# Triangular inverse of a gated DeltaNet block: one shared weight matrix per tile for two heads, transposes for the third product

## What is computed

```python
m = jnp.where(strict_lower, jnp.einsum("bhncd,bhnsd->bhncs", k_beta, k) * decay, 0.0)
t_inv = lax.linalg.triangular_solve(eye + m, jnp.broadcast_to(eye, m.shape),
                                    left_side=True, lower=True, unit_diagonal=True)
u = jnp.einsum("bhncs,bhnsd->bhncd", t_inv, v_beta)
w = jnp.einsum("bhncs,bhnsd->bhncd", t_inv, k_beta * jnp.exp(g)[..., None])
```

## Time and profile before

| | us |
|---|---|
| median of three runs | 2079.56 |
| lowest, highest | 2065.73, 2081.7 |
| span of the profiled execution | 2082.3 |
| TensorE busy | 1965.2 (94%) |
| VectorE busy | 1376.5 (66%) |
| ScalarE busy | 815.7 (39%) |
| GpSimd busy | 655.2 (31%) |
| first and last matmul of the inverse | 128.3, 659.7 |

### The profile page before, as it was taken

How to read it: one execution, slowest core, us unless ns; L and a number is a source line. 1 busy time by engine, 2 the same in 40 slices (tenths; PEclk the granted TensorE clock), 3 DMA queues, 4 the chain that set the end, 5 groups by cost and what they waited for, 6 DMA issues and landing times. The chain is left out here.

```text
span 2082.3 us, 30616 instructions
## 1 busy us (share of the span) xinstructions
PE 1965.2 (94%) x11569; PEld 1751.7 (84%) x11569; DVE 1376.5 (66%) x2764; ACT 815.7 (39%) x1260; POOL 655.2 (31%) x682
## 2 busy tenths in 40 slices
PE   8999999999998799998998989999989999999999
PEld 7776677677666588898998979999989999999999
DVE  5542542532531564299899998888667787778777
ACT  4333433433432443242433336656533333333332
POOL 4133033032031100058987841322212222222221
PEclk9999999999998899999999999999999999999999
DMA  3210210210200642259997968888779999999997
GB/s 115 79 49 21 71 37 11 71 36 21 82 16 6 230 152 89 83 150 311 309 341 263 311 197 304 311 313 307 257 253 319 319 318 322 319 319 319 320 319 239
DMA packets 147986, 411.79 MB, mean 198 GB/s; under 512 B 15616, under 2 KB 63872, under 8 KB 147328
## 3 DMA queue, kind: packets, MB, share of 16 engines
q1 hardware_dynamic: 109056, 269.31, 37.4%
q0 software_dynamic: 38784, 140.53, 20.5%
HBM read 360.23 MB, written 49.55 MB: 197 GB/s over the span
## 5 line engine op out<-in xcount | busy, mean ns | idle before, releaser
L1417 ACT ACTIVATE expert_hi<-raw 128x1024 fp32r<-128x1024 f32 x288 | 305.4, 1061 | 423.9 <-PE psE L86 392.5
L84 PE MATMUL psE<-x2h,expert_hi 128*128 128x384 f32 x1024 | 349.5, 341 | 15.3 <-POOL expert_lo L1536 14.0
L84 PE MATMUL psE<-w_hi,expert_hi 128*128 128x384 f32 x1024 | 351.2, 343 | 10.3 <-DVE expert_lo L1572 5.7
L1572 DVE TENSOR_TENSOR expert_lo<-raw,expert_hi 128x1024 fp32r<-128x1024 f32 x215 | 263.0, 1224 | 148.2 <-ACT expert_hi L1417 147.2
L85 PE MATMUL psE<-x2l,expert_hi 128*128 128x384 f32 x1024 | 344.8, 337 | 0.0
L86 PE MATMUL psE<-x2h,expert_lo 128*128 128x384 f32 x1024 | 344.8, 337 | 0.0
L86 PE MATMUL psE<-w_hi,expert_lo 128*128 128x384 f32 x1024 | 344.0, 336 | 0.0
L85 PE MATMUL psE<-w_lo,expert_hi 128*128 128x384 f32 x1024 | 343.9, 336 | 0.0
L1530 POOL DMA_INDIRECT few_gathered<-in_peer_v,picked_expert x128 | 133.5, 1043 | 429.4 <-DVE few_y L1763 388.3
L1530 POOL DMA_INDIRECT few_gathered<-in_peer_u_rows,picked_expert x128 | 151.9, 1187 | 261.0 <-DVE few_gathered L1756 235.2
L1536 POOL TENSOR_TENSOR expert_lo<-raw,expert_hi 128x1024 fp32r<-128x1024 f32 x73 | 184.8, 2532 | 132.5 <-ACT expert_hi L1417 130.6
(11 more groups left out here) (295 smaller groups left out, 3521.2 us busy)
## 6 DMA issues: line engine op xcount, KB each, us to landing
raw<-in_peer_u SPq DMA_DIRECT2D x128, 512.0 KB
raw<-in_peer_v SPq DMA_DIRECT2D x128, 512.0 KB
expert_acts<-gelu SPq DMA_DIRECT2D x124, 192.0 KB
gelu<-expert_acts SPq DMA_DIRECT2D x124, 192.0 KB, 3.1
expert_gates<-shared SPq DMA_DIRECT2D x4, 4096.0 KB, 16.5
gates_in<-expert_gates SPq DMA_DIRECT2D x32, 512.0 KB
ring<-in_w_xonly SPq DMA_DIRECT2D x24, 512.0 KB, 3.3
ring<-in_w_full SPq DMA_DIRECT2D x16, 512.0 KB, 3.9
```

Source lines behind the costliest of these rows:

```text
L84: nc.tensor.matmul(out, sh, mh, start=first, stop=False)
L1417: nc.scalar.activation(wh[:, s % R, :], raw[:, s % R, :], ACT.Copy).then_inc(S["hi_done"], 1)
L1572: v.tensor_tensor(wl[:, s % R, :], raw[:, s % R, :], wh[:, s % R, :].bitcast(F32), ALU.subtract).then_inc(S["lo_done"], 1)
```

## The change

In levels 1 to 5 the inverse of a tile consists of two 64x64 blocks on the diagonal for each head, four blocks for the two heads. The new layout keeps only these: `x0[row, tile, b, e, col]`, where for `b` = 0 the rows 0 to 63 and for `b` = 1 the rows 64 to 127 are filled. Now per tile of 128 tokens:

- **level (1 to 5):** TensorE transposes the two halves of `x0`, and makes Y for both heads in one matmul of 128 columns with one weight matrix, `ml` flattened over the heads. ScalarE makes three copies instead of one: the transposes (128x128, `pt`), and Y in two pieces of 64 rows and 64 columns each (`yp`, whose other half stays zero).
- **products (1 to 5):** one matmul of 128 columns instead of four of 64. VectorE still makes two updates, each of 64 rows and 64 columns instead of 128 and 128, and only of X; its transpose is made anew in each level.
- **level 6:** X is turned by four matmuls with the identity, Y is made for the lower left block alone by two matmuls; ScalarE makes three copies. The products are two matmuls of 64 rows and 64 columns, and VectorE makes one scaled copy instead of an update.
- **before level 0:** VectorE copies the diagonal blocks of `mtat` into `mtc`, two copies per tile.
- **masks:** GpSimd multiplies 128x128 instead of 128x256 for each tile, in levels 1 to 5; level 6 needs no mask. Once at the start it clears `yp` and copies `levels` into `levels_c`.

Tile 0 keeps its old steps, in other buffers. `UNITS` and the planner are the same.

```diff
-                        inc(nc.gpsimd.tensor_tensor(ml[0:r, l % 2, n, :, 0:r], mtat[0:r, n, :, 0, 0:r],
-                                                    both(c["levels"][0:r, l, 0:r], 2), ALU.mult), "level_ready")
+                        inc(nc.gpsimd.tensor_tensor(ml[0:r, l % 2, n, :, 0:cols], mtc[0:r, n, :, 0:cols],
+                                                    both(levels_c[0:r, l, 0:cols], 2), ALU.mult), "level_ready")
...
-                            inc(nc.scalar.activation(ys[0:r, n, :, 0:r], bank[0:r, y_bank(t), 0:2 * r].rearrange(
-                                "p (e c) -> p e c", e=2), ACT.Copy), "y_copied")
+                            y = bank[:, y_bank(t), 0:P]
+                            turned = bank[:, y_bank(t), P:4 * P].rearrange("p (b q) -> p b q", b=2)[:, :, 0:HD]
+                            whole = bank[:, y_bank(t), P:2 * P]
...
+                            elif a < LEVELS - 1:
+                                nc.scalar.activation(pt[:, n, :].rearrange("p (b c) -> p b c", b=2), turned, ACT.Copy)
+                                for e, rows in enumerate(halves):
+                                    last = nc.scalar.activation(yp[rows, n, e, :, :], y.rearrange(
+                                        "p (b e q) -> p b e q", b=2, e=2)[rows, :, e, :], ACT.Copy)
+                            else:
+                                for rows in halves:
+                                    nc.scalar.activation(xt[rows, n, :, rows], whole[rows, :].rearrange(
+                                        "p (e c) -> p e c", e=2), ACT.Copy)
+                                last = nc.scalar.activation(pt[halves[1], n, :], y[halves[1], :], ACT.Copy)
...
+                    for rows in halves if n else [slice(0, META)]:
+                        nc.vector.tensor_copy(mtc[rows, n, :, 0:rows.stop - rows.start], mtat[rows, n, :, 0, rows])
...
+                            elif a < LEVELS - 1:
+                                for b, rows in enumerate(halves):
+                                    part = half_cols(x0[rows, n, b, :, :], a, 0)
+                                    last = nc.vector.tensor_tensor(part, part, made.rearrange(
+                                        "p (e b k h) -> p e b k h", e=2, b=2, h=1 << a)[rows, :, b, :, :], ALU.subtract)
+                            else:
+                                last = nc.vector.tensor_scalar(xt[halves[0], n, :, halves[1]], made[halves[0], :].rearrange(
+                                    "p (e c) -> p e c", e=2), -1.0, None, ALU.mult)
...
-                            for e in range(2):
-                                last = mm(bank[0:r, y_bank(t), e * r:(e + 1) * r], ml[0:r, a % 2, n, e, 0:r],
-                                          xx[0:r, n, e, 0, 0:r], start=True, stop=True)
...
+                            elif a < LEVELS - 1:
+                                for b in range(2):
+                                    nc.tensor.transpose(bank[:, y_bank(t), (1 + b) * P:(2 + b) * P], flat(x0[:, n, b, :, :]),
+                                                        c["ident"][:, :])
+                                last = mm(y.rearrange("p (k h) -> p k h", h=1 << a), flat(ml[:, a % 2, n, :, :]),
+                                          half_cols(x0[:, n, :, :, :].rearrange("p b e c -> p (b e c)"), a, 0),
+                                          start=True, stop=True)
+                            else:
+                                for e in range(2):
+                                    for b, rows in enumerate(halves):
+                                        mm(whole[rows, halves[e]], x0[:, n, b, e, :], c["ident"][:, rows],
+                                           start=True, stop=True)
+                                for e in range(2):
+                                    last = mm(y[halves[1], halves[e]], mtat[:, n, e, 0, halves[1]], x0[:, n, 0, e, :],
+                                              start=True, stop=True)
...
+                            if n and a < LEVELS - 1:
+                                last = mm(made, pt[:, n, :], yp[:, n, :, :, :].rearrange("p e b q -> p (e b q)"),
+                                          start=True, stop=True)
+                            elif n:
+                                for e in range(2):
+                                    last = mm(made[halves[0], halves[e]], pt[halves[1], n, halves[e]],
+                                              xt[halves[1], n, e, halves[1]], start=True, stop=True)
```

80 lines of the change are left out of this document (55 added, 25 removed).

## The result

| | before | after |
|---|---|---|
| median of four runs | 2073.06 us | 2049.11 us |
| lowest, highest | 2065.73, 2081.7 | 2047.27, 2055.17 |
| ratio, 95% interval | | 0.9867 (0.9835 to 0.9899) |
| span of the profiled execution | 2082.3 | 2048.0 |
| first matmul of the back (psE) | 690.4 | 665.4 |

What follows compares the result with a forecast made beforehand. TensorE's issue was taken as the bound in the inverse, only just. Per pair -4.3 us, -16 over four pairs with pair 3's extras, +6 for the clock: -10, so 2070 us; own range 2058 to 2082, 8 in 10 range 2040 to 2096.

Steps and rivals of the forecast that it cites:

- the first rival: ScalarE's and VectorE's half-row pieces overlap: products near 1.2 us per level, half "level" loses nothing; 2040 us, chance 0.20.
- products, levels 1 to 5: One matmul per tile instead of four: phase ends at 1.6 us, 2.0 less per level, 10.0 less per pair.
- half "level", levels 1 to 5, with the masks: Transposes and Y: ScalarE's longer copies delay TensorE, +2.8 us per pair; smaller GpSimd masks give back 0.5.
- level 6, both halves: Identity matmuls and Y take 0.85 us per tile against 0.44, products unchanged: +1.7 us per pair.
- start: VectorE's nine new copies ahead of the first transposes are on the path: +1.7 us per pair, between 0.9 and 2.5.
- the wait ahead of the fourth tile: Sign of being right: in each half "level" TensorE waits 0.3 to 0.7 us for ScalarE's copies there.
- signs of being wrong: Transposes of 0.2 us each, clock under 0.85 in pairs 0 to 2, or cum to z over 0.5 us longer per piece.
- The rival in which the phase takes 2.6 us: Products: TensorE's freed time is all spent waiting, the change gives nothing; 2082 us, chance 0.20.
- z's waits for the exponential: In pair 3, z's waits for ScalarE's exponential grow by 1.5 us because the copies ahead of it are longer.
- The -0.5 for the masks: Smaller GpSimd masks give back 0.5 us of waiting per pair, about 1 in pair 3.
- One more drop per pair: TensorE's clock: one more short drop in each of pairs 0 to 2, about 5 us more in pair 3; +6 in all.
- The rival in which the clock makes the kernel slower: Thinner work keeps TensorE at 1.2 GHz for most of pair 3's inverse, with 15 short drops elsewhere: 2108 us, chance 0.12.

Runs made afterwards that it cites:

- four-bank kernel: Changed kernel with products of tiles 3 and 4 in PSUM banks 2 and 4, one wait for all updates per level: 2029.44 us, ratio 0.9792.
- the experiment with the later copies: Changed kernel with VectorE's nine copies of the diagonal blocks behind the first subtractions instead of ahead of them: 2045.28 us, ratio 0.9838.
- The experiments with one copy more or less: Changed kernel with one small ScalarE copy more per tile in levels 1 to 5: 2061.59 us; with Y's two copies made as one: 2051.77 us.
- both experiments that move them: Changed kernel with the nine block copies made by ScalarE: 2044.27 us, ratio 0.9858; or later by VectorE: 2045.28 us, ratio 0.9838.

## Why the prediction was right, and where its sizes were off

The outcome lies inside the range, and the mechanism was the one forecast: TensorE's issue shrinks, and handoffs come up behind it. But 24 us were gained and not 10. 2049 us is below the forecast's own range of 2058 to 2082, and only the width down to the first rival's 2040 took it in. Part of that is the base: 2070 was worked out from a median of 2079.56, which a fourth run moved to 2073.06. The change ended just beyond 1%, a case that was given a quarter of the chance. Of the first rival, one half came true by its size, that the half "level" loses next to nothing, though ScalarE's copies did not overlap as it said (0.61 us per tile, not 0.38); its products at 1.2 us did not. Term by term, per pair (lengths from pair 1 of both kernels):

| term | predicted | measured |
|---|---|---|
| products, levels 1 to 5 | -10.0 | -8.6 |
| half "level", levels 1 to 5, with the masks | +2.8 - 0.5 | +0.1 |
| level 6, both halves | +1.7 | -0.1 |
| start | +1.7 | +1.95 |
| sum | -4.3 | -6.6 |

Of the signs that were named ahead, several were missed by a little: the products take 1.90 us (1.4 to 1.8), the wait ahead of the fourth tile is 0.16 (0.3 to 0.7), the wait ahead of the first transposes 2.64 (2.2 to 2.6), the windows of the inverse in pairs 0 and 1 are 77 us long (78 to 80). None of the signs of being wrong came: a transpose takes 0.12 to 0.13 us (321.65 to 321.90 for two), the clock was 0.96, and from cum to z no piece of pair 1 takes over 0.1 us more than before.

**Products.** The prediction put tile 3 at 0.95 us and the end of the phase at 1.6. The runs gave 1.12 and 1.90. The three pieces are a first matmul with its way to VectorE of 0.53 us (0.4 taken), an update of 0.47 (0.42 taken, between bounds of which the upper was right) and a way back of 0.13 (0.1). The rival in which the phase takes 2.6 us was wrong, and so was the one in which it comes near 1.2. The gap ahead of the third matmul, which was to be seen, is there. The four-bank kernel shows that the whole of what is above 1.00 us is the handoff.

**Half "level".** This is the step that failed most. The price of the copies was taken too high, 0.74 us per tile against 0.61: two activations on 64 rows and 64 columns cost 0.43 together where 0.46 were taken, and the copy of 128 columns is followed after 0.15 to 0.18 us, where 0.28 was taken for it. More important, each level's delay was added up as if nothing gave way. At level 4, where 0.55 us was predicted, 0.31 was lost; in level 2 it was 0.1, and in level 1 the half became 0.7 shorter (4.88 us from 281.81 to 286.69 before, 4.19 from 281.43 to 285.62 after), because the wait of 0.93 us for VectorE's split of the weights, ahead of this level's steps of the projection, went away (the experiment with the later copies). In pair 3, which has no such wait, the five levels lost 1.1 us instead of 0.1. Read where they ran at full clock, level 4 takes 3.60 us instead of 3.24 there (after: in the four-bank kernel) and level 5 3.90 instead of 3.54. There, z's waits for the exponential, forecast to grow by 1.5 us, went from 5.4 to 5.9. The -0.5 for the masks found no place in these numbers: a mask takes 0.488 us instead of 0.757, yet the last tile of level 1 still waits for it. The wait ahead of the fourth tile, predicted at 0.3 to 0.7, was 0.16: at level 4 this tile's transposes started 0.38 us behind the matmul for Y ahead of it, which takes 0.22. The experiments with one copy more or less confirm that little comes through: up to 0.37 us per level for four copies of 0.2.

**Level 6.** Predicted at 0.85 us per tile, it takes 0.54: two tiles run from 342.46 to 343.54 us in pair 1, against 0.44 each before.

```profile
342.46 0.45 PE L1161 MATMUL psB<-ident,inverse 128*64 128x64 f32 x8
...
343.54 6.66 PE L1222 MATMUL psB<-norm_work,v 16*64 16x512 f32 x20
```

The first four matmuls with the identity take 0.29 us (until 342.75), 0.07 each, where 0.10 each was read from the step with 64-column weights and 128 columns; 0.25 are left for Y, near the lower end of the range that was given. The half became 0.37 us longer and the products 0.44 shorter, to which 0 had been given.

**Start.** +1.7 was predicted and +1.95 measured: a pair of copies takes 0.45 us. That VectorE's nine copies stand on the path was right, and both experiments that move them show it.

**Clock.** One more drop per pair was forecast, at 1.6 us each, and +6 in all. The drop came, but at a place that the prediction had not named, right behind the wait of the first transposes. The twelve matmuls behind it start 0.22 us apart instead of 0.12, so it costs about 1.2 us in those alone, and 1.4 us up to level 1 (5.94 us instead of 4.51). The term as a whole can't be checked better than to some 10 us, since the fronts of the kernel before alone differ by that, with 0.95 and 0.98 as mean clock: against its first execution the changed kernel has no more time at half clock (64 and 64 us), against its second twice as much (33). In pair 3 the clock was 0.87 in the first profile, which the prediction's limit of 0.85 for pairs 0 to 2 doesn't reach, and these had 0.96. The rival in which the clock makes the kernel slower is refuted.

**Sum.** Three times -6.6 and about -5.4 for pair 3 are -25 at full clock, and with an extra drop of 1.4 per pair about -20; the fronts differ by 15 to 27, by which of the four profiles are taken, and the ratios are 0.9867 and 0.9902, 28 and 20 us. So the errors of the half "level" and of level 6, 4 us per pair together, outweighed that of the products, 1.4. Both had been put well above what came, level 6 near the slow end of its bounds, and both partly for the same reason: the price of a small instruction was taken from larger ones.

## What to carry to other kernels

When a change takes issue away from the bound engine, ask for each producer and consumer how long its handoff takes and how many buffers turn; here two PSUM banks were enough for 16 matmuls of 0.22 us and too few for four, and four banks, which gave the kernel before nothing, gave the changed one 18 us in the lengths of its products of levels 1 to 5, and 28 in front and median. Small preparations on another engine are dear ahead of a wait of the bound engine and cheap beside it: nine copies cost 2 us per pair in waiting and 1.4 by the drop of the clock behind it, and moving them won both, less 0.5 to 0.7 us that came back in the next stage. A delay of a covered engine is not to be added up level by level; one or two experiments with one instruction more and one less give the share that comes through.

## What was not expected of the hardware

- A wait of 2.64 us of TensorE was followed by 3.40 us at half clock in the pair shown (1.00 to 0.50, in the windows above), and moving the copies away removed it. It repeats: the seven executions with this wait have it 28 times, and within 2 us of its end a drop begins in 26 of them; the six executions with a wait of 0.7 us there have it 24 times, and a drop begins there in none. The 1.96 us of further waiting so cost 3.4 us per pair until level 1 began.
- ScalarE's activations on 64 rows and 64 columns followed each other after 0.21 to 0.24 us, those of 128 rows and 128 columns were followed after 0.15 to 0.18, and both are shown with 0.20 to 0.28 us each: starts overlap the ends, so that three of them cost 0.61 us and not 0.69.
- The same stall of 6.2 us in the back, of TensorE for GpSimd, stood in some executions of both kernels and was absent in others. Two profiles can differ by 6 us through it alone, and the backs of the changed kernel's two executions differed by 13.
